# DeltaNet steps: decay differences on ScalarE in the rounds, query sum in another bank, output norm ahead of the value taps

## What is computed

```python
qkv = silu(causal_conv(proj[..., :GD_QKV], conv_w))        # 4 taps
g = -exp(a_log) * softplus(a + dt_bias)                     # G = cumsum(g) in a chunk
q, k = l2norm(q) * GD_DK ** -0.5, l2norm(k)                 # 8 heads; v has 16
gamma = exp(where(incl, G[:, None] - G[None, :], -inf))     # the decay differences
a_mat = where(strict, (k @ k.T) * gamma * beta[:, None], 0)
t_mat = triangular_solve(a_mat + eye, eye)
u, w  = t_mat @ (v * beta), t_mat @ (k * beta * exp(G))
qk    = (q @ k.T) * gamma
# per chunk: v_new = u - w S;  o = (q exp G) S + qk v_new;  S = decay S + k_g.T v_new
o = rmsnorm(o) * gain * silu(z);  return o @ w_out
```

## Time and profile before

| | |
|---|---|
| median of 3 runs | 2401.43 us (2399.4 to 2401.56) |
| the profiled execution's own time | 2400.58 us |
| its span | 2398.7 us |
| PE busy | 2296.8 us, 96% of the span |
| DVE busy | 1276.2 us, 53% |
| ACT busy | 979.9 us, 41% |
| POOL busy | 430.1 us, 18% |
| mean granted PE clock | 0.979 |
| DeltaNet steps 1 to 7 | from 1529.46 to 1900.88 us of the span |

### The profile page before, as it was taken

How to read it: one execution, slowest core, us unless ns; L and a number is a source line. 1 busy time by engine, 2 the same in 40 slices (tenths; PEclk the granted TensorE clock), 3 DMA queues, 4 the chain that set the end, 5 groups by cost and what they waited for, 6 DMA issues and landing times.

```text
span 2398.7 us, 31764 instructions
## 1 busy us (share of the span) xinstructions
PE 2296.8 (96%) x11326; PEld 1865.2 (78%) x11326; DVE 1276.2 (53%) x1544; ACT 979.9 (41%) x1351; POOL 430.1 (18%) x330
## 2 busy tenths in 40 slices
PE   8999998999999999999999998888999999999997
PEld 7888886788778888878888876666777887888885
DVE  5454336666464544355544358866666635554433
ACT  5232334555442323343323337455554633423332
POOL 2121101111121211021211021225311112121100
PEclk9999999999999999999999999899999999999998
DMA  5322331222223332323332322211222122332332
GB/s 161 103 90 91 91 104 62 80 78 70 71 70 105 96 92 83 96 81 112 91 102 79 96 89 74 62 54 54 62 78 65 51 90 61 105 102 91 84 96 65
DMA packets 68588, 203.16 MB, mean 85 GB/s; under 512 B 8320, under 2 KB 12544, under 8 KB 68512
## 3 DMA queue, kind: packets, MB, share of 16 engines
q1 hardware_dynamic: 68512, 202.13, 27.8%
HBM read 199.94 MB, written 2.16 MB: 84 GB/s over the span
## 4 chain that ended last, share of the span: by engine, by line
PE 86%; DVE 8%; ACT 5%; issue 1%; DMA 0%; SPq 0%; DVEq 0%; ACTq 0%
PE bank L1690 71%; PE bank L1901 7%; DVE resid L1014 1%; DVE attn L1270 1%; DVE h_lo L999 1%; DVE y L1009 1%; DVE w_lo L995 1%; ACT w_hi L523 1%; PE bank L2053 1%; PE bank L2030 1%; ACT h_hi L547 0%; PE bank L1862 0%; DVE sq L1248 0%; DVE gd_o L1251 0%; DVE gate L1198 0%
## 5 line engine op out<-in xcount | busy, mean ns | idle before, releaser
L995 DVE TENSOR_TENSOR w_lo<-raw,w_hi 128x1024 fp32r<-128x1024 f32 x405 | 584.0, 1460 | 485.5 <-ACT w_hi L523 485.5
L1690 PE MATMUL bank<-h_hi,w_hi 128*128 128x512 f32 x1720 | 686.1, 399 | 39.2 <-DVE h_lo L999 32.5
L1690 PE MATMUL bank<-h_hi,w_lo 128*128 128x512 f32 x1720 | 675.4, 393 | 0.0
L1690 PE MATMUL bank<-h_lo,w_hi 128*128 128x512 f32 x1696 | 666.1, 393 | 0.0
L523 ACT ACTIVATE w_hi<-raw 128x1024 fp32r<-128x1024 f32 x405 | 426.1, 1055 | 547.9 <-PE bank L1690 531.7
L1690 PEld LDWEIGHTS bank<-h_hi,w_hi 128*128 128x128 f32 x1720 | 326.9, 190 | 116.6 <-issue 33.2
L1690 PEld LDWEIGHTS bank<-h_hi,w_lo 128*128 128x128 f32 x1720 | 326.6, 190 | 69.6
L1690 PEld LDWEIGHTS bank<-h_lo,w_hi 128*128 128x128 f32 x1696 | 322.7, 190 | 68.8 <-issue 3.1
L1555 POOL TENSOR_TENSOR y<-y,up 128x512 f32<-128x512 f32 x88 | 173.9, 1976 | 745.7 <-DVE up L1038 671.2
L1690 PE MATMUL bank<-act_hi,w_hi 128*128 128x512 f32 x704 | 277.4, 394 | 0.0
L1690 PE MATMUL bank<-act_hi,w_lo 128*128 128x512 f32 x704 | 276.0, 392 | 0.0
(11 more groups left out here) (264 smaller groups left out, 2362.3 us busy)
## 6 DMA issues: line engine op xcount, KB each, us to landing
raw<-in_ffn_in SPq DMA_DIRECT2D x172, 512.0 KB, 3.5
raw<-in_gd_in SPq DMA_DIRECT2D x49, 512.0 KB, 3.5
raw<-in_ffn_out SPq DMA_DIRECT2D x64, 384.0 KB, 3.1
raw<-in_ffn_out SPq DMA_DIRECT2D x64, 320.0 KB, 2.9
raw<-in_hg_in SPq DMA_DIRECT2D x32, 512.0 KB, 3.5
raw<-in_gd_out SPq DMA_DIRECT2D x16, 512.0 KB, 3.7
raw<-in_hg_out SPq DMA_DIRECT2D x8, 512.0 KB, 3.5
g_bc<-g_rows SPq DMA_DIRECT2D x8, 512.0 KB, 5.4
```

What stands on the lines that cost most here:

```text
L995: nc.vector.tensor_tensor(w_lo[:, r, :], raw[:, r, :], w_hi[:, r, :].bitcast(f32), ALU.subtract).then_inc(lo_split, 1)
L1690: ins = nc.tensor.matmul(dst, w, moving[ml][:, k, :], start=first and n == 0 and (wl, ml) == (0, 0), stop=last and n == len(ks) - 1 and wl ...
```

## The change

- `attn` gets a second buffer, chosen by the group's parity. The decay differences of group j are now ACT's: `decays(j, e)`, a Relu with a pointer bias over 128 by 128, four for each head, placed in the rounds behind `new_value(g, 1)` and `new_value(g, 2)`. DVE's `log_gamma` is gone.
- For j >= 1 `query_sum` writes bank 6 and waits for `out_root`'s logarithm (`on_logged`) and no more for `out_norm`; `scores` waits for `out_norm` in its place. PE runs it behind 2 pieces, where there were 5, then 3 pieces, `level_p5`, one piece, and `level_t5` (there were two pieces between these). `late_key_sum` moves behind `level_p5`.
- ACT runs `value_tap(j, 0)` behind `out_root`, `gammas` and `query_root`, and no more ahead of the table load; `evict_p5` comes before the key roots and `row_gammas`; `part_of(n0 + 5)` moves behind `evict_t5`.
- DVE runs `out_norm`, `decayed_keys` and `query_norm` ahead of the value taps; `lo(n0 + 5)` moves behind `probs_out`, `lo(n0 + 6)` behind the taps of the second value head; the two transposes of step 4 move into its rounds.

The diff, cut to its core:

```diff
-            attn = part("attn", [P, TILES, P])
+            attn = part("attn", [P, 2, TILES, P])
...
-                    nc.scalar.activation(qn, bank[2][:], ACT.Ln, bias=eps[:, 0:1]).then_inc(q_logged, 1)
+                    nc.scalar.activation(qn, bank[6 if n else 2][:], ACT.Ln, bias=eps[:, 0:1]).then_inc(q_logged, 1)
...
+                def decays(n, e):
+                    act.wait_ge(g_loaded, 16 * (n + 1))
+                    wait(act, og_made, 2 * (n - 1))
...
+                    for t in range(NT):
+                        ins = nc.scalar.activation(attn[:, n % 2, e * NT + t, :], g_bc[:, e, t * P:(t + 1) * P], ACT.Relu,
+                                                   bias=tab[:, 5, t, h:h + 1], scale=-1.0)
+                    ins.then_inc(d_made, 1)
...
                     new_value(g, 1)
+                    decays(j, 0)
...
                     new_value(g, 2)
+                    decays(j, 1)
...
                     out_square(g)
                     query_square(j)
-                    value_tap(j, 0)
                     act.preload_act_table_set("natural_log_exp_and_others")
                     out_root(g)
                     gammas(j)
-                    if g == 0:
-                        key_root(4)
-                        key_root(5)
+                    query_root(j)
+                    value_tap(j, 0)
+                    evict_p5(j)
+                    if g < 2:
+                        key_root(2 * g + 4)
+                        key_root(2 * g + 5)
+                    if g == 1:
+                        lane_gamma(1)
                     row_gammas(j)
-                    part_of(n0 + 5)
...
                     value_silu(j, 0)
                     evict_t5(j)
+                    part_of(n0 + 5)
                     value_tap(j, 1)
                     values_by_token(j, 0)
+                    part_of(n0 + 6)
                     value_silu(j, 1)
...
                     residual(g, 1)
+                    if j == 4:
+                        from_lanes(1, 1)
...
                     residual(g, 2)
+                    if j == 4:
+                        from_lanes(1, 0)
...
-                    log_gamma(j, 0)
-                    log_gamma(j, 1)
                     value_drain(j, 0)
-                    value(j, 0, (1, 2))
                     out_norm(g)
                     decayed_keys(j)
...
-                    value(j, 0, (3,))
-                    lo(n0 + 5)
                     query_norm(j)
+                    value(j, 0)
...
                     value_drain(j, 1)
-                    lo(n0 + 6)
                     probs_out(j)
+                    lo(n0 + 5)
                     value(j, 1)
+                    lo(n0 + 6)
...
                 def query_sum(n):
                     pe.wait_ge(q_squared, n + 1)
-                    wait(pe, og_normed, 2 * n)
+                    wait(pe, on_logged, 2 * n)
...
                 def scores(n):
                     pe.wait_ge(qn_ready, n + 1)
+                    wait(pe, og_normed, 2 * n)
...
                     if level:
-                        piece(5)
+                        piece(2)
                         query_sum(j)
+                        piece(3)
+                        level_p5(j)
+                        piece()
                         if j in (1, 2):
                             late_key_sum(2 * j + 2)
                             late_key_sum(2 * j + 3)
-                        level_p5(j)
-                        piece(2)
+                            piece()
                         level_t5(j)
```

More of the change, by code:

```diff
@@ L153, in flat @@
             return t[:].rearrange("p a b -> p (a b)")
-        ab_in, ab_exp = flat(attn)[0:AB, 0:TOK], flat(attn)[0:AB, TOK:2 * TOK]
+        ab_in, ab_exp = [attn[:, 0, x * NT:(x + 1) * NT, :].rearrange("p a b -> p (a b)")[0:AB, :] for x in range(2)]
         keep_rows, g_step = flat(at)[0:AB, 0:TOK], flat(at)[0:AB, TOK:2 * TOK]
@@ L750, in values_by_token, with gammas @@
                     copy(vt[:, e, :, :], bank[token_bank(n, e)][:].rearrange("p (t v) -> p t v", v=P)).then_inc(vt_ready, 1)
-                def gammas(n, sign=1.0):
+                def gammas(n):
                     for e in range(2):
                         act.wait_ge(d_made, 2 * n + e + 1)
-                        gamma = attn[:, e * NT:(e + 1) * NT, :]
-                        nc.scalar.activation(gamma, gamma, ACT.Exp, scale=sign).then_inc(gam_ready, 1)
-                def first_decays():
-                    act.wait_ge(g_loaded, 16)
-                    act.wait_ge(ab_dve, 10)
-                    for e in range(2):
-                        h = head_row(0, e)
-                        for t in range(NT):
-                            ins = nc.scalar.activation(attn[:, e * NT + t, :], g_bc[:, e, t * P:(t + 1) * P], ACT.Relu,
-                                                       bias=tab[:, 5, t, h:h + 1], scale=-1.0)
-                        ins.then_inc(d_made, 1)
+                        gamma = attn[:, n % 2, e * NT:(e + 1) * NT, :]
+                        nc.scalar.activation(gamma, gamma, ACT.Exp, scale=-1.0).then_inc(gam_ready, 1)
+                def decays(n, e):
+                    act.wait_ge(g_loaded, 16 * (n + 1))
+                    wait(act, og_made, 2 * (n - 1))
+                    if n == 0:
+                        act.wait_ge(ab_dve, 10)
+                    h = head_row(n, e)
+                    for t in range(NT):
+                        ins = nc.scalar.activation(attn[:, n % 2, e * NT + t, :], g_bc[:, e, t * P:(t + 1) * P], ACT.Relu,
+                                                   bias=tab[:, 5, t, h:h + 1], scale=-1.0)
+                    ins.then_inc(d_made, 1)
                 def first_diagonal():
@@ L950, in deltanet @@
                 lane_gamma(0)
-                first_decays()
-                gammas(0, -1.0)
+                decays(0, 0)
+                decays(0, 1)
+                gammas(0)
                 row_gammas(0)
@@ L1251, in substitute, with from_lanes @@
                         TT(below, below, part, ALU.add).then_inc(lane_sub, 1)
-                def from_lanes(x):
+                def from_lanes(x, which):
                     if x == 0:
@@ L1258, in from_lanes @@
                         dve.wait_ge(base_ready, 4)
-                    nc.vector.transpose(diag[:, 1, :, :], lane_t.rearrange("p i j -> p j i")).then_inc(diag_ready, 1)
-                    nc.vector.transpose(diag[:, 0, :, :], lane_t).then_inc(diag_ready, 1)
+                    src = lane_t.rearrange("p i j -> p j i") if which else lane_t
+                    nc.vector.transpose(diag[:, which, :, :], src).then_inc(diag_ready, 1)
                 def tiles(e):
                     return slice(e * NT, (e + 1) * NT)
-                def log_gamma(n, e):
-                    dve.wait_ge(g_loaded, 16 * (n + 1))
-                    wait(dve, og_made, 2 * n)
-                    h = head_row(n, e)
-                    for t in range(NT):
-                        ins = TS(attn[:, e * NT + t, :], g_bc[:, e, t * P:(t + 1) * P], tab[:, 5, t, h:h + 1], 0.0, ALU.subtract, ALU.min)
-                    ins.then_inc(d_made, 1)
                 def decayed_keys(n):
@@ L1958, in value_transpose @@
                         pe.wait_ge(k_logged, 2 * n + 3 + e)
+                    if n and e:
+                        pe.wait_ge(q_logged, n + 1)
                     pe.wait_ge(qkv_silu, v_conv(n, e) + 1)
```

45 lines of the change are left out of this document (18 added, 27 removed).

## The result

The changed kernel takes 2384.27 us, the median of 4 runs (2383.81 to 2384.66); the kernel before took 2400.41 in 4 runs beside them (2398.77 to 2401.56). The ratio is 0.9933, with a 95% interval of 0.9916 to 0.995. The profiled execution took 2384.66 us, with a span of 2382.8. Against the profile before that is 15.9 us less, where the forecast had 18.3. Steps 1 to 7 account for 15.0 of it (371.4 us before, 356.4 now); what lies ahead of step 1 and behind step 7 is 0.9 us shorter.

What follows compares the result with a forecast made beforehand. PE bounds 86% of the span, with 16.6 us of waits before the query sum. Steps 1 to 7 sum to -19.7, plus 1.4 for the clock: -18.3 from 2400.58, a median of 2383 us, 8 in 10 between 2373 and 2394.

Steps and rivals of the forecast that it cites:

- part 1: PE's wait before the query sum goes: -1.6 us in steps 1, 2, 5, 6, 7, -4.0 and -4.8 in 3 and 4.
- part 2: Chain behind the first level, to the second value head: new waits on PE, +0.7 us in each step.
- the new waits don't show: Rival, chance 0.15: the 0.5 and 0.7 us of new waits behind the first level vanish, 8.4 in all, so 2374.
- The table load: ACT's load in the chain behind the first level: counted as 1.28 us, without the skill's added drain of about 1380 ns.
- part 3: Decay differences on ACT in the rounds: cost 0 in steps 3 to 7, +0.5 us each in steps 1 and 2.
- part 4: Step 4's transposes moved into its rounds: the state update waits for the first, +1.0 us (between 0.5 and 1.5).
- in the sum: Adding up the steps: steps 3 and 4 come to 47.9 and 48.9 us, -5.0 and -5.2, longer waits and low clock gone.
- the taps run into POOL: Rival, chance 0.06: value heads' taps slowed beside POOL's work, 5.0 us in each of seven steps, so 2417.
- part 5: Steps 1 and 2, key roots moved and part of the low clock given back: -3.6 us and -2.5 us.
- the +1.4 that I left in: Two falls of the clock, as the 0.70 us that step 7 lost, allowed for over the steps: +1.4 us.
- the clock stays as it was: Rival, chance 0.20: a stretch at 0.50 clock falls into each of seven steps, 1.3 us each, so 2392.
- Its own signs: What would show it right (no query-sum wait, steps 5 and 6 near 47.9) or wrong (48.8 or more, taps of 4 us).

Runs made afterwards that it cites:

- e3: The kernel before with only a second buffer and the decay differences on ACT in the rounds; bank, pieces and order unchanged: 2377.55 us, ratio 0.9901.
- e7: The changed kernel with ACT's copy and DVE's remainder of weight unit n0 + 5 moved behind the second value head's copy and taps: 2376.74 us, ratio 0.99.
- e4: The changed kernel with step 4's two transposes back behind the query taps: 2380.74 us, ratio 0.9917.
- e2: The changed kernel with the decay differences back on DVE, in the second buffer, ahead of the first value head: 2386.34 us, ratio 0.9939.
- e9: The changed kernel with step 4's transposes back behind the query taps, lane_decays(1) early and one weight unit behind the second head's taps: 2371.74 us, ratio 0.9872.
- e5: The changed kernel with POOL's two instructions of lane_decays(1) run ahead of assemble(1), away from step 1's second-head taps: 2379.91 us, ratio 0.9914.
- e6: The changed kernel with three added subtractions of 128 by 256 on POOL ahead of the masking in steps 5 to 7: 2384.51 us, ratio 0.9938.

## Why the prediction was right, and where its steps were off

**The wait before the query sum (part 1)** went in all seven steps, and its working held: ACT's load starts 0.02 us after the query's square, the query sum starts at 1766.39, and the logarithms end at 1765.8, so 0.6 us were to spare where the forecast had 0.5. What part 1 did not ask is whether one half of the change would do. The move of the differences alone sets the table load and the norm 1.7 us earlier in the step (23.56 to 21.88 us after its start, 26.67 to 24.99), against a wait of 1.56 (e3). I read the row of 3.54 us as one cause among several; it was enough by itself.

**The chain behind the first level (part 2).** Counted from P, 1770.11: the first head's SiLU is over at P + 4.5 (forecast 4.6), the copy of it at P + 7.3 (7.4), the second head's SiLU at P + 10.4 (10.7), the next step at P + 20.0 (20.2). The waits were 0.22, 0.15 and 0.50 where the forecast had 0.4, 0.5 and 0.7. So steps 5 and 6 came to 47.5 and not 47.9. The size was off by 0.4 us in a step on the good side. Most of the second head's part of it is the taps: the forecast took 2.65 us for three, from the earlier trace rows, and they took 2.31. The row of 2.65 was not clean, since POOL's masking runs beside those taps for 0.53 us. The cause was right: e7 removes the unit and both later waits. The rival *the new waits don't show* is refuted; they showed, smaller.

**The table load.** The next instruction starts 1.29 us after the start of either load, in the changed kernel as before, and a load with work behind it starts 0.02 us after the instruction ahead of it (1763.20 to 1763.22). The Trainium skill (ScalarE: Activation LUTs, What ACT_TABLE_LOAD costs) adds a drain of about 1380 ns to a switch; by it the first value head would be ready 1.4 us later than it was. The trace does not agree.

**The differences on ACT (part 3)** cost nothing in steps 3 to 7, as forecast. The +0.5 in each of steps 1 and 2 were wrong: within one clock course the output sums of step 1 start 24.78 us into the step in the kernel before and 24.76 in e4, and those of step 2 at 21.93 and 22.06. By e2 the move earned nothing either, once the rest of the change was there.

**The transposes (part 4)** cost 0.8 against a forecast of 1.0, at the state update, where PE stood 0.54 (e4).

**Step 3 (in the sum)** was 2.1 us longer than forecast, 49.98 for 47.9. The failing step is "steps 3 and 4 were longer by their waits and by their clock; with both gone they come to 47.9 and 48.9". The waits and the clock went, and a third thing stood there that the larger wait had covered. POOL is busy for 45.21 us of this step, and the taps take 3.15 and 3.84 us beside it in place of 2.3:

```profile
1672.38 3.15 DVE L1200 SCALAR_TENSOR_TENSOR gate<-conv_in,conv_w,gate 128x512 f32<-128x512 f32 x3
...
1680.19 3.84 DVE L1200 SCALAR_TENSOR_TENSOR up<-conv_in,conv_w,up 128x512 f32<-128x512 f32 x3
```

Both kinds of cause meet here: in e9, where the weight unit no longer stands ahead of the second head's taps, the step takes 47.31 with taps of 3.00 and 2.79. The slower taps are the mechanism of the fourth rival, *the taps run into POOL*. It is real: e5 and e6 took POOL's work away and added it in other steps; in step 3 itself it was not varied. The Trainium skill (GPSIMD Engine Reference, Specifications) names a contention of GpSimd with VectorE instructions that have two SBUF inputs, and these taps agree with it. It decides only where POOL works for long beside the taps, in steps 1 and 3, and not in all seven. The forecast's reason against it, that the taps of step 5 took 2.65 all the same, was a misreading: 2.65 already held some of it, against 2.31 alone. I had charged it as a rival of 6% and nothing in the forecast; it belonged in the sum, at up to 2 us in step 3 and 2.5 in step 1.

**Steps 1 and 2 (part 5).** Step 1 was forecast at -3.6 and came to +0.35. The old waits went as forecast (4.6 us), but new ones of 4.4 came: 1.24 before the first head, 0.15 before level_u5 and 3.02 before the second, of which 2.5 are the taps beside POOL (e5). In the kernel before those taps were slow too (4.10), and PE waited for no value head in that step; the two waits ahead of them, now gone, had covered them. The rounds took 1.6 us more, by the clock's other course, and the rest of the step 1.1 less. So the -3.6 fails in two terms: the new waits, and the clock, which was to give 0.6 back. That term was too small in itself: in e5, without the slow taps and in the course of the kernel before, step 1 is 5.3 us shorter, and only 2.7 of it are waits; for the other 2.6 the traces show 6.8 us at 1.2 GHz in the kernel before, right behind its wait of 3.1, that e5 doesn't have. Step 2 came to -1.9 for -2.5; it still holds 3.4 us at 1.2 GHz, where the forecast had counted 0.9 as given back.

**The clock.** No stretch below 1.00 lies in steps 3 to 7 of the profiled execution, so the +1.4 that I left in was not spent, and for it the rival *the clock stays as it was* is refuted there. Low stretches are left in steps 1 and 2. One execution doesn't settle it for step 3: in e5 and e6, whose step 3 has the same instructions, 3.4 us at 1.2 GHz follow its wait for the second head, and it takes 51.34 and 51.57.

Put together, against -18.3: +4.0 in step 1, +0.6 in step 2, +2.1 in step 3, -0.7 in step 4, -1.3 in steps 5 to 7 together, -1.4 for the clock and -0.9 outside the steps make -15.9, which is what was measured. That 2383 came so close to 2384.27 is partly luck: terms that were too bad by 4.3 us cancelled most of the 6.7 by which three steps were too good.

**Its own signs.** No wait before the query sum, and steps 5 and 6 near 47.9, came true. "Steps 3 and 4 within 1.5 us of them" failed for step 3 (2.5 above), the wait before level_u5 was below its 0.3 to 0.8 (0.15), and of the signs of being wrong one shows: taps of 4 us, in step 1 (4.84).

## What to carry to other kernels

When a change takes one wait away by two means at once, price each alone: the engine that stood in the way may have been late by less than either gives, and then the second only brings its own cost (e3 is faster than the whole change). A weight copy between an eviction and the last chain of a stage can cost most of its length there (0.87 us for a copy of 1.06 in e7); look for where it is hidden first. And a long wait that is removed uncovers what ran beside it, here POOL's work beside DVE's taps, so ask of every stage what else was late under that wait.

## What the runs showed of the hardware

Three taps on DVE (128 by 512, two SBUF inputs) take 2.31 us alone. In step 6 of e6 POOL works for 2.6 us of them, most of it masking, and they take 3.17; in step 1 of the changed kernel it works for 3.4 us of them, on a subtraction over 128 by 1024 and a masking, and they take 4.84. POOL gets slower too: its masking of the probabilities takes 1.22 us alone and 2.12 beside taps. The price per us beside each other is 0.3 in one case and 0.7 in the other, so it is no rate. The single instructions show what it is, in us:

| tap, and POOL's instruction | tap starts | POOL's ends | tap ends | took |
|---|---|---|---|---|
| changed kernel, step 1, first tap, L1587 | 1573.42 | 1575.28 | 1575.82 | 2.40 |
| the second, L1590 | 1575.86 | 1576.94 | 1577.47 | 1.62 |
| the third, none | 1577.51 | | 1578.26 | 0.75 |
| e6, step 6, first tap, L1649 | 1822.93 | 1823.47 | 1824.02 | 1.10 |
| the second, L1635 | 1824.06 | 1824.52 | 1825.06 | 1.00 |
| the third, L1635 | 1825.10 | 1825.56 | 1826.10 | 1.00 |

A tap that starts while an instruction of POOL runs ends 0.53 to 0.55 us after that instruction, in each of the 274 such cases in steps 1 to 7 of the twelve traces in which POOL had more than 0.22 us left; alone it takes 0.75. Of 32 maskings that start while a tap runs, 23 end 0.49 to 0.50 us after the tap, where one alone takes 0.64; in the other nine the tap comes second and ends 0.54 us after the masking. So in these traces the two take turns by whole instructions, and what a tap loses is the time that POOL's instruction still has to run, less 0.2 us: 1.65 us behind the L1587 above, which takes 2.89, and 0.25 behind a masking.

The same rounds of step 1 ran in 24.8 or in 26.4 us, at a mean clock of 0.93 or 0.81, in kernels that do the same there. With the stretch at 1.2 GHz in its second half, step 1 alone differs by 3.1 us between the changed kernel and e4. Two kernels whose difference is under some 3 us need their steps compared, and not their times alone.
